# Helper steps of a delta-rule scan moved by one place, and one key product moved up GpSimd's queue

## The reference

```python
def centred_shift(z, w):
    zp = jnp.pad(z, ((0, 0), (1, 1), (0, 0)))
    return zp[:, :-2] * w[0] + zp[:, 1:-1] * w[1] + zp[:, 2:] * w[2]
...
    def step(S, inp):
        r_t, k_t, v_t, d_t, kk_t, a_t = inp
        s_kk = jnp.einsum('bhvk,bhk->bhv', S, kk_t)
        S_new = (S * d_t[:, :, None, :]
                 - s_kk[..., None] * (kk_t * a_t)[:, :, None, :]
                 + v_t[..., None] * k_t[:, :, None, :])
        y = jnp.einsum('bhvk,bhk->bhv', S if reverse else S_new, r_t)
        return S_new, y
...
    y = ((y - mu) * lax.rsqrt(var + GN_EPS)).reshape(B, T, D_A) * p["lnx_g"] + p["lnx_b"]
```

## Time and profile before

| | |
|---|---|
| median of 3 runs | 2966.96 us |
| lowest and highest | 2966.84, 2971.82 us |
| profiled execution | 2972.55 us |
| its span | 2971.0 us |
| mean granted TensorE clock | 0.977 |
| TensorE busy | 2730.1 us (92%) |
| VectorE busy | 1173.1 us (39%) |
| ScalarE busy | 608.0 us (20%) |
| GpSimd busy | 265.3 us (9%) |

### The profile page before, as it was taken

One profiled execution on the slowest core, in us unless ns is written; L12 is line 12 of the kernel. 1 busy time (PEld: TensorE's weight loads), 2 busy tenths in 40 slices (PEclk: granted clock), 3 DMA queues, 4 the chain that ended last, 5 costly groups with the idle time before them and its releaser, 6 DMA issues. The chain is left out here.

```text
span 2971.0 us, 69541 instructions
## 1 busy us (share of the span) xinstructions
PE 2730.1 (92%) x31106; PEld 1483.0 (50%) x31106; DVE 1173.1 (39%) x2615; ACT 608.0 (20%) x1253; POOL 265.3 (9%) x282
## 2 busy tenths in 40 slices
PE   6999999999989999979998989989987999999998
PEld 3567766766664445434333443433433555455553
DVE  4565556556633763172210221212013255423333
ACT  2324232433221100010000000000002344322222
POOL 1221122122200000010000000000000111110000
PEclk9999999999999999989999999999998999999999
DMA  5000000000006772358999999999994421042210
GB/s 206 25 27 21 17 24 26 21 21 18 33 5 255 285 265 74 121 234 341 430 430 431 431 430 431 430 431 430 431 430 188 147 59 37 0 132 64 59 39 29
DMA packets 188812, 557.41 MB, mean 188 GB/s; under 512 B 29452, under 2 KB 117026, under 8 KB 163958
## 3 DMA queue, kind: packets, MB, share of 16 engines
q1 hardware_dynamic: 188534, 553.19, 47.4%
HBM read 550.65 MB, written 2.24 MB: 186 GB/s over the span
## 5 line engine op out<-in xcount | busy, mean ns | idle before, releaser
L2336 PE MATMUL bank<-arena,xe 128*64 128x512 f32 x1024 | 348.4, 605 | 34.9 <-DMA gates<-in_exp_w_dram 24.4
L2336 PEld LDWEIGHTS bank<-arena,xe 128*64 128x64 f32 x1024 | 108.8, 139 | 185.3 <-issue 172.9
L673 PE MATMUL bank<-arena 128*128 128x512 f32 x384 | 192.7, 622 | 1.2 <-issue 1.2
L3360 PE MATMUL bank<-arena 128*128 128x512 f32 x384 | 175.3, 604 | 1.9 <-PEq L2655 1.9
L2336 PE MATMUL bank<-arena,hidT 128*64 128x512 f32 x512 | 171.6, 599 | 1.0 <-DMA gates<-in_exp_w_dram 0.8
L2788 PE MATMUL bank<-arena 128*128 128x512 f32 x320 | 145.1, 602 | 1.2 <-ACT arena L2936 1.2
L2336 PE MATMUL bank<-mg_ring,xe 128*64 128x512 f32 x256 | 119.2, 621 | 20.6 <-DMA u<-in_exp_w_dram 20.6
L2555 DVE TENSOR_TENSOR x<-x,bank 128x512 f32<-128x512 f32 x64 | 43.6, 686 | 228.5 <-PE bank L2374 228.5
L2548 DVE TENSOR_TENSOR hid<-hid,bank 128x512 f32<-128x512 f32 x32 | 19.8, 682 | 285.8 <-PE bank L2336 285.8
L2336 PE MATMUL bank<-ys,xe 128*64 128x512 f32 x256 | 114.5, 601 | 16.4 <-DMA arena<-in_exp_w_dram 15.7
L1539 DVE TENSOR_TENSOR pm<-bank,m_level 128x512 f32<-128x512 f32 x120 | 82.8, 690 | 103.1 <-PE bank L752 102.4
(11 more groups left out here) (523 smaller groups left out, 5484.8 us busy)
## 6 DMA issues: line engine op xcount, KB each, us to landing
arena<-in_exp_w_dram SPq DMA_DIRECT2D x96, 2048.0 KB, 26.8
gates<-in_exp_w_dram SPq DMA_DIRECT2D x24, 2048.0 KB, 29.2
ys<-in_exp_w_dram SPq DMA_DIRECT2D x24, 2048.0 KB, 26.7
mg_ring<-in_exp_w_dram SPq DMA_DIRECT2D x24, 2048.0 KB, 25.4
u<-in_exp_w_dram SPq DMA_DIRECT2D x24, 2048.0 KB, 29.9
ws_w<-in_ada_w_dram SPq DMA_DIRECT2D x40, 1024.0 KB, 5.5
arena<-in_odd_w_in_dram SPq DMA_DIRECT2D x32, 512.0 KB, 4.0
arena<-in_w_in_dram SPq DMA_DIRECT2D x24, 512.0 KB, 3.9
```

What stands on the lines that cost most here:

```text
L673: last = mm(to[:], wj[:, c, i, :], hT[:, c, 0:T], start=(c == 0), stop=(c == KT - 1))
L2336: r[e] = mm(out[a, :], lhs[j][:, a], w[:, j, 512 * c:512 * c + 512], start=(first and j == 0), stop=(last and j == len(lhs) - 1), skip_gro ...
L3360: last = mm(o[:], w[:, i, t, :], hT[:, t, :], start=(t == 0), stop=(t == KT - 1))
```

## The change

Nothing is computed differently and no instruction is added or left out. Steps change places:

- TensorE at (0,4,1): the first piece of the projection of keys and values (four channels, L669) goes ahead of `center`.
- ScalarE: `deviation(a)` goes from (1,0,0) to (1,0,1), behind the copy of U; `part_moved(j, 2)` goes ahead of `square(b)`; `blend(b)` goes from (2,0,0) to (2,0,1), behind the copy of U.
- GpSimd: `scaled_k(j + 1, 1)` goes ahead of `xt0(j + 1, 0)`.
- VectorE: `parts(j, 11)` goes from (1,3,1) to (1,3,0), ahead of the third tap of keys and values; the third tap of V goes from (2,4,1) to (0,0,0) of the following turn, behind mask and parts; `inverse_deviation(a)` goes from (1,0,0) to (1,0,1); `gated(a)` from (1,3,0) to (1,3,1).

```diff
@@ -1002,8 +1002,8 @@
                     to_tokens(j, "K", 0)
                 if at == (0, 4, 1):
                     context_of(b, 1)
+                    project(b, K_V, 0)
                     center(a)
-                    project(b, K_V, 0)
                 if at == (1, 0, 0):
                     variance(a)
                 if at == (1, 0, 1):
@@ -1363,8 +1363,8 @@
                     centered(a)
                 if at == (1, 0, 0):
                     tokens(j, "V", 1)
+                if at == (1, 0, 1):
                     deviation(a)
-                if at == (1, 0, 1):
                     widen_rstd(a)
                 if at == (1, 1, 0):
                     tokens(j, "B", 1)
@@ -1373,8 +1373,8 @@
                 if at == (1, 3, 0):
                     tokens(j, "V", 2)
                 if at == (1, 3, 1):
+                    part_moved(j, 2)
                     square(b)
-                    part_moved(j, 2)
                     root(b)
                 if at == (1, 4, 0):
                     tokens(j, "B", 2)
@@ -1389,8 +1389,8 @@
                         f(spare[:, t, 0:512], bank[o][:], ACT.Copy).then_inc(S["ahead_moved"], 1)
                 if at == (2, 0, 0):
                     tokens(j, "K", 2)
+                if at == (2, 0, 1):
                     blend(b)
-                if at == (2, 0, 1):
                     grow(b, 0)
                     shrink(b, 0)
                 if at == (2, 1, 0):
@@ -1522,8 +1522,8 @@
                 xt0(j, 2)
                 new_k(j + 1)
                 scaled_k(j + 1, 0)
+                scaled_k(j + 1, 1)
                 xt0(j + 1, 0)
-                scaled_k(j + 1, 1)
                 r_times_k(j + 1)
                 reverse_v(j + 1, 1)
 
@@ -1720,9 +1720,11 @@
 
             def beside(j, at):
                 a, b = j - 1, j + 1
-                if at[0] < 2 and at[1] < 4 and at[2] == (1 if at[0:2] == (1, 3) else 0):
+                if at[0] < 2 and at[1] < 4 and at[2] == 0:
                     parts(j, 4 + 4 * at[0] + at[1])
                 if at == (0, 0, 0):
+                    if j:
+                        shift(j, V_X, (2,))
                     params(b)
                 if at == (0, 1, 1):
                     bonus(j)
@@ -1732,9 +1734,8 @@
                     shift(b, K_X, (1,))
                 if at == (0, 3, 1):
                     shift(b, K_X, (2,))
-                if at == (1, 0, 0):
+                if at == (1, 0, 1):
                     inverse_deviation(a)
-                if at == (1, 0, 1):
                     running_sums(b, 0)
                 if at == (1, 1, 1):
                     normed(a)
@@ -1744,8 +1745,8 @@
                     shift(b, K_V, (1,))
                 if at == (1, 3, 0):
                     shift(b, K_V, (2,))
+                if at == (1, 3, 1):
                     gated(a)
-                if at == (1, 3, 1):
                     clamp(b)
                 if at == (1, 4, 0):
                     invert(b)
@@ -1770,7 +1771,7 @@
                     scaled_b(b, 1)
                     scaled_q(b, 1)
                 if at == (2, 4, 1):
-                    shift(b, V_X)
+                    shift(b, V_X, (0, 1))
 
             def low_shift(f):
 
```

## The result

The change made the kernel slower: 2980.87 us (median of 12 runs) against 2971.98 (12 runs of the kernel before, on the same chip), ratio 1.0027, 95% interval 1.0015 to 1.0038. The profiled execution took 2978.78 us, its span 2977.2 (before 2972.55 and 2971.0), with the same mean granted clock, 0.977. The scan ends 4.5 us later, at 916.22 instead of 911.67; what follows it takes 2061.0 instead of 2059.3.

A forecast was written before the change was run, and what follows sets the result against it. TensorE sets the pace, so its idle time counts: gains -20.3, new stall +8.9, clock -1.5 make -12.9 us. From the profiled 2972.55 that gives 2959.65, or 2954.0 as a median of runs, range 2945 to 2962.

The forecast's parts named there:

- the sentence on the square and the gated output: Near (1,3): square behind the parts, gated output behind the state update, both hidden in helpers' idle time; cost nothing.
- rival 4: New 1.27 us stalls in seven turns bring clock falls and make the kernel slower, 2979.4 us; chance 0.05.
- Step 11's parts: At (1,4): early mask and parts ahead of the square remove eight TensorE waits, gain 12.6 us before overlaps and clock.
- All gains together: Sum of TensorE idle spells removed over the scan, 17.7 us, plus 2.6 for overlapping starts: 20.3 us.
- rival 1: GpSimd's second half of the keys costs nothing where it now stands, out of ZG's way; 2945.2 us, chance 0.10.
- The keys: Second half on GpSimd stalls ZG and the (2,2) mask, cost 8.9 us; products opening turns gain 1.5 us.
- ZG 1.5 us: Sign: VectorE's ZG at (2,1) takes about 1.5 us instead of 0.29, held by GpSimd's step.
- Blend: At (2,0), blend behind the copy of U: what the readout gains, the mask of (2,1) loses; worth nothing.
- Centering, U, tap: TensorE waits removed: centering product 2.1 us, readout behind U at (1,0) 1.0, mask at (0,0) 0.5.
- Clock, -1.5: With the (1,4) idle spell gone its clock fall may go too: 0 to 3.1 us, half taken.
- Turns 1 to 3 shorter by 1 to 2 us each: Sign in the scan: each of these turns should shorten by 1 to 2 us.
- Rival 3: At (1,4) the mask or ScalarE's queue becomes the wait, losing half of 12.6 us and its overlap; 2960.8, chance 0.08.

The follow-up runs named there:

- the two runs that moved the boundaries: Changed kernel with 60 or 120 more TensorE instructions (satisfied waits) ahead of turn 0: 2971.59 us (1.0022) and 2968.56 us (1.0012).
- the channel put first: Changed kernel with one more channel of the projection of r ahead of the squares on TensorE: 2978.78 us, ratio 1.0039.
- the fastest kernel: Changed kernel with both the gated output and the keys' second half put back in their places: 2949.02 us, ratio 0.9937.

## Why the prediction was wrong

It said 2954.0 (2945 to 2962), against a median of 2966.96: ratio 0.9956. The kernel without one step of the change does just that (0.9958); the whole change is 1.0027. **The step that failed is the sentence on the square and the gated output: "Both are costed at nothing; without that cover the square's reader on TensorE would wait up to the 1.27 us by which it is late".** It looked at the square's reader behind ScalarE's square alone. But that reader waits for two things, and the second is the scratch bank that the gated output frees. How `Scratch` hands out its banks was in front of me; I did not follow which use of a bank the moved step releases. It costs 20.5 us (changed kernel against the one with it back):

- 4.4 us of waits of the squares in turns 1 to 6, 0.27 to 1.13 each, and 1.7 at the product of turn 7 (the waits above). Of the 0.87 in turn 3, 0.60 comes from ZG, held by GpSimd's early step on XT: another edit of the same change makes this one worse.
- 7 to 8 us of late program blocks: 2.63, 2.46, 2.12, 1.01, 0.94, 0.92 at (1,4) for 0.73, 0.70, 0.96 and nothing over 0.2. Shown by the two runs that moved the boundaries and by the channel put first.
- The rest, 6 to 7 us, is mostly the clock, which falls to 0.50 behind the spells of turns 1 to 3 (275.62 to 279.03, 374.61 to 381.43, 477.01 to 480.42). Over the whole scan it is at 0.50 for 20.5 us, and for 6.8 us with the gated output back; the 13.7 us between are these three stretches, and as an estimate half clock costs at most half of them, 6.8 us. Lined up by instruction, the stretch from 196 to 400 behind the squares takes 3.0 us longer in turn 2 of the changed kernel; the last correction alone, from its first start to its last end, takes 2.0 us (377.50 to 379.48) instead of 1.2. In turns 4 to 6, where no spell is over 1.2 us, the same stretch loses little but the spell (1.3, 1.2 and 1.0 us), and from 576 to 580 the clock is 1.00.

I had named the clock as rival 4, with the new stall of 1.27 us as its trigger. The trigger was another: no fall stands behind the seven stalls of up to 1.1 us, and one stands behind each of the spells of 2.1 to 2.6 us. Length alone does not tell in between: a fall follows a spell of 1.46 us that ends at 213.63, and none follows those of 1.42 and 1.46 that end at 316.91 and 817.47. That rival 4's time, 2979.4, is close to the measured 2980.87 is luck.

The other steps, each by its own run:

- **Step 11's parts**, -15.0 with overlaps and clock: -15.4 (0.9948, interval 12 to 19). Right. Some 3.5 us of it may be luck: the spells at block boundaries fell from 15.3 to about 12 us in that run, and no term held them.
- **All gains together**: rival 1's sum is -21.8, of which 1.9 (1.5 and four overlaps) hang on the keys' move, which the fastest kernel does not have. So -19.9, and it is 18.7 below (0.9937), interval 14 to 24. Right.
- **The keys**: +8.9 and -1.5, so +7.4: 6.2 and 7.1, and 7.2 us of waits at (2,2). Right, a little less than said. No run shows the port of the expectations' wording; what the runs show in its place is a ZG that ends 0.13 to 0.15 us behind the GpSimd step within which it starts. "L1489 of 1024 columns right behind that of 512", "ZG 1.5 us" (1.76 at (2,1), 1.56 at (2,2)), a distance of 6.51 for 5.98 (+0.53, 0.55 said): all seen. That ZG at (2,1) is 1.76 is 0.2 to 0.3 more than I worked out, and so the mask of (2,1) is 0.48 us late in turns 3 to 6: that is the 2.3 us of waits in the fastest kernel.
- **Blend: nothing.** Right within the noise (0.9944 and 0.9937, with intervals that overlap).
- **Centering, U, tap:** L950's waits are gone, L921's are 1.1, and the three small mask waits that open a turn are gone. Right as far as waits tell; no run moves these steps alone.
- **Clock, -1.5:** no run shows this term. Its bound of 3.1 us was my estimate, half of the 6.11 us that TensorE is busy at a granted clock of 0.50 in the earlier trace rows. In its place, the fall of turn 7 is 3.4 us long in the changed kernel instead of 6.8, worth at most 1.7 by the same estimate. The number is near by luck: the spell of 2.98 did not go, one of 1.74 for the gated output took its place.
- **Turns 1 to 3 shorter by 1 to 2 us each**: turn 3 is 2.9 us longer. Wrong, and it is a sign that I had named.

Rival 3, "another wait takes the place at (1,4)", had the right place and chance 0.08, but looked only at the mask and ScalarE, and had half of 12.6 as its price. I overlooked a mechanism of this size because I took a wait for what it lasts. The list of waits shows blocks of the program only as "issue", and the 1.27 us were a bound on the wait, not on what hangs behind it.

## What to carry to other kernels

Before you move a step, ask what it frees, not only what it makes: find each wait on the semaphore it raises, bank releases included, and the next use of that bank. And a wait at which an engine with a long unrolled program stands can cost more than its idle time. Here the block of program behind such a wait started to arrive 1.0 to 2.0 us after the wait opened and ran 2.2 to 2.8 us after that; behind waits of the squares of 0.27 to 1.13 us stood spells of 0.92 to 2.63 us, and behind those of 2.1 to 2.6 us the clock was 0.50 for 3.4 to 6.8 us. When a spell says "issue", count its instruction modulo 256 (202 to 204 in all 22 here), or see whether a packet of the instruction queue started 2.2 to 2.8 us before it ends, before looking for a partner.

## What the hardware showed that was not expected

- TensorE's program arrives in blocks of 256 instructions (237 packets of 16,384 bytes), and idle spells of up to 2.6 us with the releaser "issue" stand at the boundaries (22 of 22 over 0.35 us in the changed kernel's turns; 15.3 us in all in the kernel before, where "issue" also hides the waits for XT). From the start of a packet to the first instruction of its block it is 2.2 to 2.8 us. Where the sequencer asks for a block is bracketed. In turns 1 to 3 with 60 more instructions the boundary lies 117, 137 and 157 behind the squares' wait: the packet starts 2.4 to 3.1 us before the gated output ends, and there is no spell. Where it lies 177 or more behind, in all turns of the changed kernel and turns 4 to 6 of that one, the packet starts 1.0 to 2.0 us after. So the block is asked for between 157 and 177 instructions ahead of its first, by this one kernel.
- In turn 2 the block behind the squares starts 3.86 to 4.14 us behind the gated output's end in all five kernels where that step is late, whether the array idled at the wait (0.26 to 0.83 us) or not at all.
- A satisfied wait cost TensorE's sequencer 40 to 50 ns: 240 of them left the array idle 12.6 us, 120 of them 5.5, where 0.70 stood without them.
- ZG, with both operands in SBUF, ends 0.13 to 0.15 us behind the GpSimd step within which it starts, in all five places looked at, all in turn 3 ((1,3), (2,1) and (2,2) of the changed kernel, (2,2) with the keys alone, (2,1) in the earlier trace rows). Its own 0.29 us is not added.
